# A fused transformer-layer kernel on one core: attention periods placed between a dense step and the splitting of the weights that the step sets free

## The reference

```python
x = layer_norm(x, ln_in_g, ln_in_b)
z = x @ w_in                                        # 1024 x 3088, split by columns
go = gated linear attention of 4 heads (dk 64, dv 128), normed and gated
so = sb_attention(q, k, v)                          # 4 heads x 64, strictly causal
co = cb * causal_depthwise_conv3(cc * ch)           # 256 channels
mix = concat([go, so, co]) @ w_out                  # 1024 x 1024
x = layer_norm(alpha * x + mix, ln1_g, ln1_b)
x = layer_norm(alpha * x + square(relu(x @ w_up)) @ w_down, ln2_g, ln2_b)   # 1024 x 4096 x 1024
```

## Time and profile before

| | us |
|---|---|
| median of 3 executions | 3113.41 |
| lowest and highest | 3110.74, 3117.24 |
| the profiled execution's own time | 3112.73 |
| its span in the profile | 3110.9 |
| PE busy | 2734.4 (88%) |
| DVE busy | 1505.1 (48%) |
| ACT busy | 1069.5 (34%) |
| POOL busy | 329.9 (11%) |
| mean granted TensorE clock | 0.934 of full speed |

### The profile page before, as it was taken

The page is one execution under the profiler, slowest core; times in us unless marked ns, Lnnn a source line. Parts: engine busy times, 40 slices in busy tenths (PEclk is TensorE's granted clock), DMA queues, the critical chain, the costliest instruction groups (busy, mean ns, idle before and its releaser), DMA issues. The chain is left out here.

```text
span 3110.9 us, 38667 instructions
## 1 busy us (share of the span) xinstructions
PE 2734.4 (88%) x13838; PEld 2268.3 (73%) x13838; DVE 1505.1 (48%) x2247; ACT 1069.5 (34%) x1783; POOL 329.9 (11%) x283
## 2 busy tenths in 40 slices
PE   5999999946662467999998999999999988999997
PEld 4787789835541356888877888877888766888885
DVE  5333342158883556665656544446644425522224
ACT  3323333223342424443443444443434321322221
POOL 1100010056600000000001100001100000000000
PEclk9999999966786588999999999999999989999998
DMA  5544454233315654575655766565766554544452
GB/s 185 169 160 153 160 180 126 85 121 88 89 45 187 191 191 140 169 249 179 216 193 191 229 218 209 191 206 183 234 190 227 170 171 144 190 157 158 154 168 98
DMA packets 362107, 526.11 MB, mean 169 GB/s; under 512 B 28832, under 2 KB 208208, under 8 KB 361920
## 3 DMA queue, kind: packets, MB, share of 16 engines
q1 hardware_dynamic: 337696, 480.23, 48.1%
q10 hardware_dynamic: 18832, 26.10, 2.3%
q0 software_dynamic: 5392, 17.31, 1.6%
HBM read 422.74 MB, written 100.80 MB: 168 GB/s over the span
## 5 line engine op out<-in xcount | busy, mean ns | idle before, releaser
L111 PE MATMUL p_ps_u<-p_xh,p_wh 128*128 128x512 f32 (+1 forms) x1280 | 453.1, 354 | 5.4 <-DVE p_xl L1626 5.4
L112 PE MATMUL p_ps_u<-p_xh,p_wl 128*128 128x512 f32 (+1 forms) x1280 | 451.5, 353 | 0.0
L113 PE MATMUL p_ps_u<-p_xl,p_wh 128*128 128x512 f32 (+1 forms) x1280 | 451.0, 352 | 0.0
L1575 DVE SCALAR_TENSOR_TENSOR p_res<-p_res,p_ps_d 128x512 f32<-128x512 f32 (+1 forms) x340 | 232.1, 685 | 451.4 <-PE p_ps_d L113 445.7
L111 PE MATMUL p_ps_d<-p_wh,p_hh 128*128 128x512 f32 (+1 forms) x1088 | 433.2, 398 | 16.9 <-DVE p_res L1575 14.8
L112 PE MATMUL p_ps_d<-p_wh,p_hl 128*128 128x512 f32 (+1 forms) x1088 | 428.6, 394 | 0.0
L113 PE MATMUL p_ps_d<-p_wl,p_hh 128*128 128x512 f32 (+1 forms) x1088 | 428.4, 394 | 0.0
L1484 ACT ACTIVATE p_wh<-p_wst 128x1024 fp32r<-128x1024 f32 x288 | 293.9, 1049 | 276.6 <-PE p_ps_d L113 225.0
L1633 DVE TENSOR_TENSOR p_r<-p_r 128x512 f32<-128x512 f32 (+1 forms) x160 | 95.8, 599 | 461.3 <-ACT p_hh L1514 461.3
L1507 ACT ACTIVATE p_r<-p_ps_u 128x512 f32<-128x512 f32 (+1 forms) x160 | 83.8, 524 | 579.5 <-PE p_ps_u L113 579.4
L111 PEld LDWEIGHTS p_ps_u<-p_xh,p_wh 128*128 128x128 f32 x1280 | 241.2, 188 | 35.5 <-DVE p_xl L1626 6.2
(11 more groups left out here) (155 smaller groups left out, 4473.0 us busy)
## 6 DMA issues: line engine op xcount, KB each, us to landing
p_wl<-wlo_scratch SPq DMA_DIRECT2D x216, 512.0 KB, 5.1
p_wst<-in_w_up SPq DMA_DIRECT2D x128, 512.0 KB, 6.0
p_wst<-in_w_down SPq DMA_DIRECT2D x128, 512.0 KB, 4.6
wlo_scratch<-p_wl SPq DMA_DIRECT2D x72, 512.0 KB, 3.6
p_wst<-in_w_in SPq DMA_DIRECT2D x128, 256.0 KB, 3.6
p_kk<-ks_scratch SPq DMA_DIRECT2D x84, 256.0 KB, 5.9
p_vv<-vs_scratch SPq DMA_DIRECT2D x84, 256.0 KB, 4.5
p_wst<-in_w_out SPq DMA_DIRECT2D x32, 512.0 KB, 6.0
```

Source lines behind the costliest of these rows:

```text
L111: pe.matmul(out, lhs_hi, rhs_hi, start=first, stop=False, skip_group_check=skip)
L112: pe.matmul(out, lhs_lo, rhs_hi, start=False, stop=False, skip_group_check=skip)
L113: return pe.matmul(out, lhs_hi, rhs_lo, start=False, stop=last, skip_group_check=skip)
L1575: dve.scalar_tensor_tensor(out=acc, in0=acc, scalar=scale, in1=ps_d[:c, d % DB, :], op0=ALU.mult, op1=ALU.add).then_inc(d_free, 1)
```

## The change

split_weights(i) is no longer called right behind the dense step but at the end of the loop's body, behind add_attention. Where both put something after the same dense step, the order is now dense step, attention, splits, and was dense step, splits, attention. Nothing else is edited.

```diff
@@ -1249,7 +1249,6 @@
                 add_attention(group_end[st[1]])
             if st[0] in ("up", "down", "out"):
                 order.append(st)
-                split_weights(i)
             elif st[0] == "mix":
                 order.append(st)
                 if st[2] + 4 < KT:
@@ -1259,6 +1258,8 @@
             spent += price[i]
             if i < mixed[-1]:
                 add_attention(begun + int((len(periods) - 1 - begun) * spent / sum(price)))
+            if st[0] in ("up", "down", "out"):
+                split_weights(i)
         assert put == len(periods) - 1 and next_w == len(wunits)
```

## The result

The changed kernel took a median of 3123.57 us (3120.12 to 3124.81, 6 executions), the kernel before in the same comparison 3113.67 us. The ratio is 1.0031, with a 95% interval of 1.0018 to 1.0044: slower by 9.9 us, or 0.3%. The forecast was 3122. The profiled execution took 3124.39 us with a span of 3122.3, that of before 3112.73 with 3110.9.

The account below looks back on a forecast made before the run. PE was taken to bound phase_tail, busy 299.99 of 300 us between 1700 and 2000. Losses 12.2 plus clock 6.4 minus gains 9.7 gave +8.9 on 3112.7, with the median's 0.7 3122 us; range 3118 to 3127, 8 in 10 3105 to 3132.

Parts of the forecast that it names:

- Where PE waits, and that it does not for weights: In phase_tail, attention waits a split could lengthen total 20.4 us; no PE wait is for p_wh, p_wl or weight DMA.
- Gains: Attention no longer behind a split in phase_tail: 3.2 + 2.2 + 0.7 + 2.0 + 1.6 = 9.7 us gained.
- The clock term of 1.6: At PE's p_ob wait at 2489.28 us, a gap cut to 2.0 avoids the half-clock stretch: 1.6 us gained.
- Losses: Low-half reloads behind the period's DMAs on SP, five places, plus a home unit's low half on DVE: 12.2 us lost.
- v_load + 0.76 + landing: On SP, a reload goes 0.76 us behind the period's v_load and takes 3.9 us to land.
- the third rival: Longer landings: at 5.1 us or more each of five places is 1.2 later, +16.5, 3129 to 3130 us; chance 0.10.
- All others that I followed keep some slack: Reloads followed other than the five listed at 1717 to 2346 us were taken to arrive in time, without loss.
- The clock: Behind four new PE gaps of 2.2 us or more the clock falls to 0.50: 4 x 1.6 = 6.4 us lost.
- The sum: Whole kernel: 12.2 + 6.4 - 9.7 = +8.9 us; forecast chance 0.47.
- That of the reloads nearly in time: Reloads land in 3.5 us with half or no clock loss: +0.5 to +3.7, some 3115 us; chance 0.28.
- the fit of the Trainium skill: Transfer as 2.0 us plus bytes over 436e3, for the GpSimd path: 3.2 us per 512 KB reload, about 3115 us.
- The faster one: Attention's waits on p_atl and p_ob vanish altogether: 27.8 gained against 18.6 lost, -9.2, or 3104 us; chance 0.12.

Follow-up runs that it names:

- second profile of the changed kernel: The changed kernel run again without further edits, beside the shorter filling: 3124.88 us, ratio 1.0034 to the kernel before (3114.73 us).
- the changed order for the others alone: Changed order for the 216 units after the first 72, order of before for those 72 home units: 3134.16 us, ratio 1.0062 to the kernel before.
- the filled runs: Changed kernel plus extra unread PE matmuls before units 87, 95, 103, 132: 3122.07 us with 18, 9, 10, 15; 3123.72 us with 16, 7, 8, 13.
- the shorter filling: Changed kernel plus 16, 7, 8 and 13 extra unread PE matmuls before units 87, 95, 103 and 132: 3123.72 us, ratio 1.0021 to the kernel before.

## Why the prediction was right, point by point

- **Where PE waits, and that it does not for weights:** right. The gains lay in those rows, and the losses behind SP, with the clock behind both.
- **Gains.** The wait at 1212.71 went as a whole; that at 1236.8 fell from 1.51 to 0.38 (forecast 1.2 gained, measured 1.1); both for p_aw and the one at the score matmul went; 3.42 fell to 2.69 (forecast 0.6, measured 0.7); p_ob fell from 3.98 to 2.09, where I said 2.0 would stay. The row is

```profile
2505.59 0.26 PE L1822 MATMUL p_ps_o<-p_ath,p_vv 64*128 64x64 f32 x1 [2.09 <-DVE p_ob L1694]
```

  The clock term of 1.6 was wrong in its reason. I expected no slow stretch behind a wait of 2.0 us, and it came: the granted clock over 3 us from 2507 us is 0.53, and some 8 matmuls start 0.43 us apart where some 11 did before, so 0.7 us were won at this place and not 1.6. In the second profile of the changed kernel nothing was won there (0.50 over 3 us from 2503.1). That 6.8 us were won from 2480 to 2570 us in the first profile is luck: there the waits of 1.81 and 2.69 us at 2548.64 and 2569.98 had a clock of 1.00 behind them, and in the second profile the same two had the slow stretch, and 2.3 us were won. The two shorter waits alone explain 2.6.
- **Losses.** "v_load + 0.76 + landing" held at each of the five places: the reload is 0.76 us behind the v_load every time. Landing, from the issue to PE's start, was 3.8 us at units 95, 132 and 183, 4.2 at unit 103 and 4.9 at unit 87, for 3.9 in the forecast. For unit 28 the profile shows idle time without a releaser; by the starts 0.4 us were lost there.

| unit | wait, forecast | wait, measured |
|---|---|---|
| 87 | 3.1 | 3.98 |
| 95 | 2.2 | 1.84 |
| 103 | 2.2 | 2.18 |
| 132 | 3.5 | 3.19 |
| 183 | 0.9 | 0.54 |
| home unit 28 | 0.3 | 0.18 |
| 73 | none | 2.48 |

  That 3.9 fitted owes something to luck. "Of several such, 3.6 to 4.0" names the quick ones: of the 28 reloads that the kernel before issues right behind a v_load, ten land within 4.0 us and the slowest takes 7.6, with a median of 5.1. From that median the third rival would have followed. In the changed kernel there are 38 such reloads, and their median is 3.8 us. Why they land sooner was not tested.

- **The step that was missed** is "All others that I followed keep some slack". At the seam of groups 0 and 1 two reloads and two loads of w_out come one right behind the other, with a k_load:

```profile
1602.64 0.32 SPq L1391 DMA_DIRECT2D p_wl<-wlo_scratch  x1
1603.05 0.38 SPq L1379 DMA_DIRECT2D p_wst<-in_w_out  x1
1603.62 0.33 SPq L1391 DMA_DIRECT2D p_wl<-wlo_scratch  x1
1604.04 0.38 SPq L1379 DMA_DIRECT2D p_wst<-in_w_out  x1
...
1612.70 0.59 PE L111 MATMUL p_ps_d<-p_wh,p_xh 128*128 128x512 f32 x1 [2.48 <-DMA p_wl<-wlo_scratch]
```

  The second reload took 8.9 us from 1603.62 to land. The wait and the slow stretch behind it cost 4.3 us; the other 1.2 of the 5.5 in the table were lost behind the 6.1 us that PE stands still at 1580 us, and are lost in the second profile too. That is the mechanism of the third rival, at one place. In the second profile of the changed kernel the same four loads are issued within 0.02 us of the same times, the second reload lands in 6.3 us, and PE does not wait for it. So this wait comes and goes from one execution to the next, with the landing and not with the order.
- **The clock.** Four waits at 1.6 us each, 6.4 in all. Measured, 19.3 us were lost from 1700 to 2020 us, 11.2 of them waits; the other 8.1 make 2.0 for each. In the second profile it is 20.4 and 11.7, so 2.2 for each, and with the changed order for the others alone 17.1 and 11.3, so 1.9 for each of the three stretches that came. Mechanism right, and the size measured a quarter or more above the forecast. With the open point of the filled runs this holds for the profiles only.
- **The sum** was +8.9. The medians differ by 9.9 (10.2 in the later comparison) and the two traces by 11.4. That the sum came so near is in part luck, for its terms missed in both directions and made up for each other: losses larger by 1.9 from 1700 to 2020, by 0.7 in its neighbours and by 5.5 at the seam, gains larger by 0.9 and 2.6 in the two stretches that had them, and 2.0 us that the stretch up to 1190 us, in which nothing was edited, happened to give.
- **The rivals.** That of the reloads nearly in time fell (3.8 to 4.9 us to PE's start, and the clock did fall). That of the longer landings held at the seam alone. By the fit of the Trainium skill (DMA: Bandwidth & Descriptors, "Anatomy of one DMA — SWDGE (gpsimd) path") a landing would be 3.2 us as an estimate; none of the five was as short, and the page states it for another path than SP's. The faster one fell as well: the waits for p_atl lost 3.3 us in all, and that for p_ob kept 2.1.

## What to carry to other kernels

When one written order feeds several engines, moving an entry moves it in every queue, and each queue has its own answer: here the order on ACT and DVE, with the w_loads behind it, gave 11 us (3102.2 against 3113.5), and the place of the reloads on SP's queue cost 21 (3123.6 against 3102.2). Take the entry apart before it is moved: what waits for little (a load whose slot is already free) goes ahead of what waits for long, and the version with the reloads alone left in place is 11 us faster than the kernel before. To find such a place, read the waits of the engine that issues the DMAs: a long wait at a line says what everything behind it on that queue will have to stand through.

## What the runs showed that was not expected

- Whether the clock falls behind a wait is not told by the wait's length here. Behind a wait of 3.98 us some 11 matmuls ran at 0.50 of full speed, and behind waits of 1.84 and 2.18 us the clock fell too. But 2.12 us at 1647 us had a clock of 1.00 behind it in the changed kernel's first profile and the same wait at 1643 us 0.50 in the second; 1.84 us at unit 103 had 1.00 behind it with the changed order for the others alone; and a wait of 1.5 us at 1193 us had 1.00 behind it in the kernel before, and the same wait, 1.4 us at 1195, had 0.50 behind it in the profile of the shorter filling. A forecast can price such a stretch, but for waits of this size it has to give its coming a chance.
- Keeping PE busy in the waits removed the slow stretches in two profiles (clock 0.97 to 1.00 over 340 us, 6.8 and 8.3 us saved there) and took only 1.2 to 1.5 us off the medians. A saving read from one profile need not be one of the kernel, and executions that scatter by 9 us need many repeats to show 7.
